# First block: ScalarE reads a projection's bank before it rounds the next weight unit, not after it

## The reference, cut to what matters

```python
for l in range(DEPTH):                       # DEPTH = 2
    proj = x @ w_in[l]
    hq, hf, hi, hg, nq, kc, vc, ks, vs, kw, vw, gt = jnp.split(proj, pts, axis=-1)
    o_a = hgrn2_mixer(hq, hf, hi, hg, lbs[l], hg_norm_w[l])     # 4 heads of 128, gated recurrence
    o_b = nsa_mixer(nq, kc, vc, ks, vs, kw, vw, gt, ...)        # 8 heads of 64, sparse attention
    mix = jnp.concatenate([o_a, o_b], axis=-1) @ w_out[l]
    x = layer_norm(ALPHA * x + mix, ...)
    ffn = (jax.nn.silu(x @ w_ffn_gate[l]) * (x @ w_ffn_up[l])) @ w_ffn_down[l]
    x = layer_norm(ALPHA * x + ffn, ...)
```

## Time and profile before

| what | value |
|---|---|
| runs of the kernel, median | 1686.91 us |
| the profiled execution | 1685.33 us |
| its span, first to last instruction | 1683.5 us |
| PE busy | 1622.6 us (96%) |
| ACT busy | 917.3 us (54%), 518.3 us of it the 510 high parts of L689 |
| DVE busy | 1152.7 us (68%) |
| POOL busy | 444.1 us (26%) |
| mean granted PE clock | 0.995 of full speed |

### The profile page before, as it was taken

How to read it: one execution, slowest core, us unless ns; L and a number is a source line. 1 busy time by engine, 2 the same in 40 slices (tenths; PEclk the granted TensorE clock), 3 DMA queues, 4 the chain that set the end, 5 groups by cost and what they waited for, 6 DMA issues and landing times.

```text
span 1683.5 us, 30215 instructions
## 1 busy us (share of the span) xinstructions
PE 1622.6 (96%) x11354; PEld 1477.5 (88%) x11354; DVE 1152.7 (68%) x1633; ACT 917.3 (54%) x1576; POOL 444.1 (26%) x184
## 2 busy tenths in 40 slices
PE   8989999999988999999999999999999999999997
PEld 7888799988877899978899989999788999899996
DVE  5687754457787554476784877776758857777767
ACT  5664554446645544465655564455765556554545
POOL 2122122212221222224511122232235311223222
PEclk9999999999999999999999999999999999999999
DMA  9542455646424655546323455665564333466663
GB/s 333 168 126 95 163 202 187 202 161 215 161 72 137 225 190 194 187 160 221 127 95 120 141 186 193 218 202 189 171 209 153 111 101 129 164 212 211 215 197 123
DMA packets 82563, 288.74 MB, mean 172 GB/s; under 512 B 9051, under 2 KB 11908, under 8 KB 81924
## 3 DMA queue, kind: packets, MB, share of 16 engines
q1 hardware_dynamic: 77352, 272.58, 48.6%
q10 hardware_dynamic: 5084, 14.37, 2.6%
HBM read 284.81 MB, written 2.11 MB: 170 GB/s over the span
## 4 chain that ended last, share of the span: by engine, by line
PE 63%; DVE 6%; ACT 2%; issue 2%; DVEq 0%; ACTq 0%
PE bank L727 30%; PE bank L744 26%; PE bank L1301 2%; DVE w_lo L693 1%; PE bank L1282 1%; PE bank L1273 1%; PE bank L1261 1%; PE bank L772 1%; ACT w_hi L689 1%; PE bank L1314 0%; PE bank L781 0%; DVE small L2566 0%; DVE z L2522 0%; PE bank L917 0%; PE bank L925 0%
## 5 line engine op out<-in xcount | busy, mean ns | idle before, releaser
L693 POOL TENSOR_TENSOR w_lo<-raw,w_hi 128x1024 fp32r<-128x1024 f32 x146 | 380.4, 2606 | 1138.7 <-ACT w_hi L689 1138.7
L693 DVE TENSOR_TENSOR w_lo<-raw,w_hi 128x1024 fp32r<-128x1024 f32 x364 | 555.7, 1551 | 146.7 <-ACT w_hi L689 144.8
L689 ACT ACTIVATE w_hi<-raw 128x1024 fp32r<-128x1024 f32 x510 | 518.3, 1051 | 88.7 <-PE bank L744 44.1
L727 PE MATMUL bank<-x_t_hi,w_hi 128*128 128x256 f32 x1984 | 316.9, 282 | 2.3 <-ACT p_t L556 1.6
L727 PE MATMUL bank<-x_t_hi,w_lo 128*128 128x256 f32 x1984 | 307.6, 277 | 0.0
L727 PE MATMUL bank<-x_t_lo,w_hi 128*128 128x256 f32 x1984 | 307.0, 277 | 0.0
L727 PEld LDWEIGHTS bank<-x_t_hi,w_hi 128*128 128x128 f32 x1984 | 270.1, 189 | 14.2 <-issue 5.1
L727 PEld LDWEIGHTS bank<-x_t_hi,w_lo 128*128 128x128 f32 x1984 | 264.5, 188 | 0.0
L727 PEld LDWEIGHTS bank<-x_t_lo,w_hi 128*128 128x128 f32 x1984 | 263.0, 188 | 0.0
L744 PE MATMUL bank<-w_hi,x_t_hi 128*128 128x512 f32 (+3 forms) x448 | 133.6, 381 | 7.3 <-issue 3.4
L744 PE MATMUL bank<-w_hi,x_t_lo 128*128 128x512 f32 (+3 forms) x448 | 131.5, 376 | 1.9 <-DVE x_t_lo L1983 1.9
(11 more groups left out here) (390 smaller groups left out, 2099.7 us busy)
## 6 DMA issues: line engine op xcount, KB each, us to landing
raw<-stream SPq DMA_DIRECT2D x511, 512.0 KB, 4.3
rows<-rows ACTq DMA_DIRECT2D x4, 1024.0 KB, 4.5
gain<-rows ACTq DMA_DIRECT2D x8, 512.0 KB, 3.9
hv_p<-hv_dram ACTq DMA_DIRECT2D x14, 256.0 KB
x<-x_in SPq DMA_DIRECT2D x2, 512.0 KB, 5.1
bias_r<-rev_dram SPq DMA_DIRECT2D x1, 1024.0 KB, 7.2
hv_dram<-hv ACTq DMA_DIRECT2D x2, 512.0 KB, 7.7
y_out<-x SPq DMA_DIRECT2D x2, 512.0 KB, 2.7
```

What stands on the lines that cost most here:

```text
L689: self.eng.activation(w_hi[:, i, :], raw[:, i, :], ACT.Copy).then_inc(hi_done.sem, 1)
L693: self.eng.tensor_tensor(w_lo[:, i, :], raw[:, i, :], w_hi[:, i, :].bitcast(F32), ALU.subtract).then_inc((lo_pool if self.part == "pool" e ...
L727: mm = pe.matmul(target, a[:, i, w0 + kt * P:w0 + (kt + 1) * P], b[:, k0 + kt, :], start=kt + k == 0, stop=k == 2 and kt == kts - 1)
```

## The change

At 18 places of a layer of the first block, ACT now reads the projection's bank first and makes the high part of the unit six ahead second. Nothing is added or removed, and all other engines' orders stay as they are. The three helpers that all 18 places go through are changed: `projected` (ks, hf0 to hf3, kw, hg0 to hg3), `sparse_query` (nq0 to nq3) and `query` (hq0 to hq3).

```diff
                 def projected(name, target):
+                    read_bank(at, name, target, lambda b: b[:, 0:S])
                     split.ahead(uid[name])
-                    read_bank(at, name, target, lambda b: b[:, 0:S])
 
                 def sparse_query(j):
 
                     name = f"nq{j}"
-                    split.ahead(uid[name])
                     act.wait_ge(*banks.full(at, name))
                     act.activation(nq[:, j, :], bank[banks.bank(at, name)][:, 0:S], ACT.Copy, scale=-0.125
                                    ).then_inc(*banks.frees(at, name))
+                    split.ahead(uid[name])
 
                 def query(h):
 
                     name = f"hq{h}"
-                    split.ahead(uid[name])
                     act.wait_ge(*banks.full(at, name))
                     act.activation(hq[:, h, :], bank[banks.bank(at, name)][:, 0:S], ACT.Copy, scale=lbc[:, 8 + h:9 + h]
                                    ).then_inc(*banks.frees(at, name))
+                    split.ahead(uid[name])
```

## The result

The changed kernel took 1692.42 us in the median of 22 runs (1687.98 to 1697.3), the kernel before 1687.10 in 22 runs beside it (1682.91 to 1690.95). The ratio is 1.0030 with a 95% interval of 1.0022 to 1.0039: about 5 us slower, where I had forecast 1687.3 and no measurable change. The profiled execution took 1689.62 us (span 1687.8, mean granted clock 0.993), against 1685.33 (1683.5, 0.995).

A forecast was written before the change was run, and what follows sets the result against it. PE's own work was taken as the bound, 63% of the wait chain. Layers at 0.0 with end terms -0.35 and +0.25, doubled, plus 0.35 for hf0 gave +0.35 us on 1686.91: 1687.3 us, range 1684.0 to 1692.0.

The forecast's parts named there:

- hf0: Layer 1: the pass now precedes ACT's read of p0, so PE starts hf1 0.35 us later; layer 0 unchanged.
- hf3 and kw: Passes behind these reads delay L1560 by 0.73 us and kw by 0.31; PE starts hq1 1.04 us late.
- hq1, hq3: Earlier hq3 read and DVE's L2223 freed from POOL's low part: PE at hg0 between -0.35 and +0.46, taken +0.05 us.
- The port: First decays: DVE's q_e (L2109) goes in before POOL's low part, so cross scores come 1.6 us earlier per layer.
- POOL keeps its turn: Slower rival: POOL's low part directly follows k_e(1), q_e ends 2.35 us later; 1691.9 us, chance 0.25.
- hg1: Compressed scores wait for masked("cross") behind the moved pass and DVE's low part: PE +0.66 us per layer.
- hg2: The pass now stands between the read and decay_exp(3), with nothing to hide it: +0.95 us per layer.
- the zero per layer: Per layer, first decays, compressed scores and decay_exp(3) sum as -1.6 + 0.66 + 0.95 = 0.0 us.
- if any stretch outside 40 to 175 and 400 to 530 us changes its length, I have missed a path: Sign in the changed kernel's timeline: length changes only within those two stretches, otherwise a path was missed.
- The weight stream: Passes come later everywhere, but PE wants those units six units on, some 18 us: 0 us.

The follow-up runs named there:

- hg1 alone: Against the kernel before, only place hg1 reads the bank first: 1690.79 us, ratio 1.0018.
- taken out of the change: Against the changed kernel, DVE's masked("cross") stands ahead of its low part of unit hg1 + 6: 1687.95 us, ratio 0.9999 to the kernel before.
- hg1 to hg3: Against the kernel before, only the places hg1, hg2 and hg3 read the bank first: 1694.26 us, ratio 1.0042.
- hg2 alone: Against the kernel before, only place hg2 reads the bank first: 1688.08 us, ratio 1.0004.
- ks to kw: Against the kernel before, only ks, nq0 to nq3, hf0 to hf3 and kw read the bank first: 1687.47 us, ratio 1.0004.
- hq0 to hq3 with the mask first: Against the kernel before, hq0 to hq3 read first and DVE's masked("cross") precedes its low part of unit hg1 + 6: 1681.57 us, ratio 0.9969.
- the fill experiment: Against the changed kernel, three needless PE products in the standstill ahead of level_scores(5): 1694.23 us, ratio 1.0041 to the kernel before.
- the late mask: Against the kernel before, three needless DVE copies ahead of the copy in masked("cross"): 1689.03 us, ratio 1.0016.
- hg0: Against the kernel before, only place hg0 reads the bank first: 1686.94 us, ratio 0.9996.
- hq0 to hq3 with hg0 (again): Against the kernel before, only hq0 to hq3 and hg0 read first, repeated with more rounds: 1682.97 us, ratio 0.9971.
- the mask first and POOL's order moved: Against the kernel before, hq0 to hq3 read first, masked("cross") precedes DVE's low part, POOL's hg0 + 6 low part follows decayed_k(2): 1686.37 us, ratio 0.9987.

## Why the prediction was wrong

The trace bears out most steps, and the sum is wrong all the same. Point by point, for layer 1:

1. *hf0.* PE began hf1 at 415.48 for 414.93, +0.37 net of what it came with. Predicted 0.35.

2. *hf3 and kw.* hq1 at +1.47, net of the start +1.3. Predicted 1.04; the wait in front is one of 1.95 us for p_t.

3. *hq1, hq3.* hg0 at +0.14, predicted +0.05. L2223 became 1.68 us for 3.82, and the scans behind it took 4.00 us for 2.62, beside POOL's low part that now began at 458.87: the block moved on, as written.

4. *The port.* Right in mechanism and size: L2109 1.00 us, cross scores and hg1 at -1.49, predicted -1.6. The rival "POOL keeps its turn" forecast 1691.9, next to the measured time, but its mechanism didn't occur: L2109 would have been over 3 us. A time that fits doesn't show a reason.

5. *hg1.* L1074 waits 0.69 us for a mask straight behind a low part, and PE goes from -1.49 to -0.81, +0.68 for the predicted 0.66. As written in the trace; as a term of the sum +1.3, where the runs give 2.7 (hg1 alone) and 2.4 to 2.9 (taken out of the change) at equal clock, and 3.5 and 3.6 to 4.5 in the medians.

6. *hg2.* The exponential starts 1.23 us behind the read, and PE's level_scores(4) came from -0.83 to +0.02, +0.85. Predicted 0.95.

Up to 505 us PE is thus at +0.1 against before, and the zero per layer that I summed stands there in the trace. One step failed for certain, and the price of one term is in doubt.

**The sum has no term for the clock.** I added waits to 1686.91 and left PE's own products at the length they had. That number stood 1.58 us above the profiled execution, whose clock was 0.995 where the runs have 0.9929 in the mean, and I carried the 1.58 over as if it were fixed; for the changed kernel it is 2.80 (1692.42 against 1689.62). The mean granted clock over the runs fell from 0.9929 to 0.9907 and 0.9909. At 0.94 us for each 0.001 that is 2.0 us of the 4.1 to 4.8 by which the means differ. The trace shows the places: the stretch at 506.5 left PE 1.2 us later in a part of the program that has no slack to give it back, those at 731.8 and 1216.5 some 0.7 and 1.5. That is 3.4 of the 4.3 us by which this profile is longer.

Whether the change brought these stretches is suggested and not shown. At 506 and 1216 the kernel before waited as long and kept its clock. But the second profile of the changed kernel has the stretch again at 508.0, and one at 733.2. In the 17 profiles kept, half speed begins at this place of the ladder in six: the change twice, hg1 to hg3 (513.6), hg2 alone (507.5), ks to kw (509.7), and hq0 to hq3 with the mask first (502.0). The Trainium skill, "TensorE: Matmul & The Clock Gate", section "HAM oscillation — how this bites in real kernels", warns that a PE which stands still for data starts again at half clock. The rows above agree that half speed came right behind standstills, and also show one of 2.0 us without it. What makes the one or the other stays open: the fill experiment didn't settle it.

**The price of item 5.** The traces put the wait at 0.7 to 0.8 us a layer, near the forecast, and the runs with hg1 alone put it at 2.7 at equal clock (1.9 to 3.6), those with the late mask at 1.8. The traces suggest one thing that the sum lacks. In the 17 profiles L1074 runs 34 times. PE waits ahead of it for a mask in 16, by 0.33 to 0.78 us, and behind 5 of these the clock falls to half speed 2.0 to 3.1 us after L1074's start: hg1, hg0, hq0 to hq3 with hg0 (again), the late mask, and the fill. Behind the 18 without a wait it never does. Each of the five cost PE 1.6 us against before. No run was made to test this, and the changed kernel's two profiles don't have a stretch there.

Of the 2.2 to 2.7 us that the change costs at equal clock, 0.35 was forecast, and 1.1 to 1.6 would be item 5's excess over its 1.3. The rest, some 0.3 to 1.2 us, is not accounted for. The clock and the waits are not cleanly apart either. In layer 0 the profile of before has a half-speed stretch at 122.3, exactly where q_e was blocked. PE would have waited there anyway, and the stretch cost it 0.6 us, by the late-mask kernel, whose q_e was blocked there at full clock. That also hides a wait of before: the waits in 30 to 175 us are 12.2 us in before and 14.2 after, though q_e was freed.

My sentence "if any stretch outside 40 to 175 and 400 to 530 us changes its length, I have missed a path" points at the fault: from 530 us to the end the profile grew by 3 us, with waits of 19.1 us before and 19.2 after. The weight stream, to which I gave 0, held. Of the 3 us, 2.2 lie in the half-speed stretches at 731.8 and 1216.5, and the rest in neither waits nor such stretches.

## What to carry to other kernels

Decide for each place, not for the helper: read first where somebody waits for the bank and nobody soon for the pass (hq0 to hq3, 0.3 to 0.4% faster in four kernels, though only 0.1% in a fifth, with the mask first and POOL's order moved), and leave the pass first where a third engine's in-order queue has it ahead of something that TensorE wants (hg1). Where an edit makes another engine's instruction late, look at what stands behind it in that queue: moving the mask one place forward gave back the change's whole loss. Look also at what an operation that is moved out of one's way meets next: POOL's low part met the third q_e.

Where PE is 96% busy, a sum of waits is not the time: read the granted clock of every run beside it, compare kernels at equal clock, and allow for 2 us of it in 1690 in the range.

## What the runs showed of the hardware

*Who gets the shared port.* When one of DVE and POOL waits and the other has its next operation queued, the waiting one goes next. Rows 8 show POOL going in between two of DVE's; with POOL's old order, all 18 places where q_e was issued before k_e(1) ended show DVE going in between two of POOL's, with q_e at 0.85 to 1.03 us, and all 12 where it came later show 2.2 to 2.7. In before q_e came 0.2 us after the end of k_e(1), in the changed kernel 0.45 ahead of it, and that decided some 1.6 us. The scans (L2236) took 4.00 us for 2.62 with POOL's low part beside them.

*The clock of a busy kernel.* A program that is 96% busy on PE had 4 to 8 stretches at 1.2 GHz in each of 17 profiles, most of them some 3.4 us long, about 0.9 us of the total each on average and from 0.6 to 1.6 by place. Their places recur in part: of the seven of one profile of the changed kernel, a second has six within 1.5 us, and has two others. Between kernels that differ only in their order the mean clock ranged from 0.9900 to 0.9946, which is over 4 us, more than most of the waits that this study set out to move.
